# A two-part f32 kernel: the last output tiles of its first attention layer split into latent and context parts, and products of ones ahead of the input's transposes

## The chip, the cores and the metric

The kernel runs on one core of a Trainium2 chip. The metric is the device time of one execution in microseconds, as the median of several runs. In the text PE is the matmul engine (TensorE), PEld its weight loads, DVE is VectorE, ACT is ScalarE, POOL is GpSimd, and SP is the engine whose queue issues most of the DMA. PSUM is the accumulator memory of PE, in eight banks (`ps[:, 0]` to `ps[:, 7]`).

## The reference, cut to what matters

The whole computation is a gated block and after it two attention layers, A and B, on 512 latent tokens (`x`) and 256 context tokens (`ctx`), 1024 channels. The change lies at the start of the first block (norm of the input) and between the layers:

```python
for i in range(2):                                   # layer 0 is mixer A, layer 1 mixer B
    h  = modulate(x,   g_norm, shift,   scale)       # rmsnorm(x, g) * (1 + scale) + shift
    hc = modulate(ctx, g_norm, shift_c, scale_c)
    y, yc = mixer(h, hc, ...)
    x = x + gate[:, None] * y
    if not last:
        ctx = ctx + gate_c * yc
# end of mixer A:   y = (o * silu(g)) @ w_o ;  yc = (oc * silu(gc)) @ w_o
# start of mixer B: cq, ckv, kr, g = split(h @ w_in) ; ckv_c, kr_c = hc @ w_in[:, part]
```

The norm of a token needs the squares of all of its 1024 channels, so nothing of `h` can be made before the last output tile of mixer A is there.

## The kernel before

**Layout and precision.** Activations lie transposed, channels in the 128 partitions and tokens along the row, in KT = 8 tiles of 128 channels. Each f32 product is made of three fast ones: both operands are split in a high and a low part (`w_hi`, `w_lo`, `h_hi`, `h_lo`), and high by high, high by low and low by high are accumulated in PSUM. The high part of a weight strip (128x2048, 256 output channels) is a copy on ACT (helper `hi`, L748), the low part a difference on POOL in pieces of 512 columns (helper `lo`, L1267). There are two slots of `raw`, `w_hi` and `w_lo`. `hi` waits on `s_proj` until the slot's last products are done.

**Start.** ACT squares the four tiles of the input (L764), DVE and ACT make the norm's root and scale the tiles, and PE turns them with 32 transposes (L2164) after two small turns of parameter rows (L2155, L2156), which wait for the small loads (`s_const`). The transposes go over two token halves for k = 0 to 7, twice: the eighteenth is the first that completes a channel tile. ACT then makes `h_hi` tile by tile (L778), DVE `h_lo` (L1459), and PE the first projection (L2182 to L2184).

**End of layer A.** For each of eight output tiles m (phase `a_out`, L2565 to L2581) PE issues for each of 8 channel tiles three products of 512 columns (latent) and three of 256 (context), into banks 2j and 2j + 1 with j = m % 2, and signals `s_proj` once. DVE adds the tile to the residuals `x1T` (L1979) and `xcT` (L1980) and signals `s_free`; ACT squares both (L1111, L1112, helper `e_square`), and DVE sums the squares up to tile 6 (L1973, L1974, `s_esum`). ACT places the high parts of the next strips between the squares.

**Norm and layer B.** After the eighth tile PE sums over channels (L2586, helper `e_stat`: one-column products of `e_sum`, `e_csum` and the last squares with `ones`), DVE makes mean and reciprocal (L1987 to L1989), ACT the root (L1127), and PE spreads the roots over the partitions with transposes (L2390, helper `spread`). Then `h` of layer B is made tile by tile: DVE multiplies (L1772, `mod_t`), ACT scales and shifts twice, once into PSUM and once rounded into `h_hi` (L987, L988, `mod_hi`; for k = 0, 3, 6 DVE does the first, L1775), DVE subtracts into `h_lo` (L1780, `mod_lo`). PE takes each tile k as it comes, with six products of 512 columns for two output tiles of `cq` (L2449 to L2451, `weigh3`), then the latent products of the second strip of phase `b_in`, then those of the context.

The order on each engine is the order in which the code is written; there is no scheduler. Semaphores carry counts: phase objects (`Phase`, L518 to L520) hold the count at which a phase starts (`t0`).

Of the kernel before, what the change touches and what calls it, by code (L numbers as in the profile page):

```python
# [112 lines left out]
def block_kernel(nc, t):  # L113

    ctx = ExitStack()
    with ctx:
# [622 lines left out]
        def _(act):  # L739
# [367 lines left out]
            def e_square(k):  # L1107
# [15 lines left out]
            for k in range(5, KT):
                e_square(k)
            hi(b_in, 0, 1)
            act.wait_ge(s_einv, 1)
            nc.scalar.activation(e_st[:, 2, :], e_st[:, 1, :], ACT.Sqrt).then_inc(s_eroot, 1)  # L1127
            for k in range(KT):
                mod_hi(2 * KT + k, k, S, h_hi[:, k, :], 1, 0)
# [306 lines left out]
        def _(dve):  # L1436
# [532 lines left out]
            def e_sums(k):  # L1969
# [3 lines left out]
                v.tensor_tensor(e_sum[:, :], e_sum[:, :], tmp[:, k % 2, :], ALU.add)  # L1973
                v.tensor_tensor(e_csum[:, :], e_csum[:, :], e_csq[:, k % 2, :], ALU.add).then_inc(s_esum, 1)  # L1974

            for k in range(KT):
                j = k % 2
                dve.wait_ge(s_proj, a_out.t0 + k + 1)
                v.scalar_tensor_tensor(x1T[:, k, :], ps[:, 2 * j, :], ada_a[:, 2, k, 0:1], x1T[:, k, :], ALU.mult, ALU.add)  # L1979
                v.scalar_tensor_tensor(xcT[:, k, :], ps[:, 2 * j + 1, 0:C], ada_a[:, 2, k, 1:2], xcT[:, k, :],  # L1980
                                       ALU.mult, ALU.add).then_inc(s_free, 1)
# [851 lines left out]
```

## Time and profile before

| | us |
|---|---|
| median of 3 runs | 1522.52 |
| the three runs | 1522.37, 1522.52, 1525.46 |
| the profiled execution | 1521.91 |
| its span on the core | 1520.1 |
| PE busy | 1467.2 (97% of the span) |
| DVE, ACT, POOL busy | 788.6, 670.2, 556.8 |
| mean granted clock of PE | 0.989 of full speed |

The span is what the trace covers, from the first instruction to the last; 1.8 us of the profiled execution lie around it. In a timeline row, the first number is the start in us from the span's start, the second the duration of the merged rows, and what stands in brackets is how long the engine had been idle and what ended that. PEclk is the granted clock of PE: 1.00 is 2.4 GHz, 0.50 is 1.2 GHz. A row `x8` merges eight records. An f32 product that is not a transpose leaves two records, so that four products are `x8`.

### The profile page before, as it was taken

What the parts mean: (1) busy time and instruction counts of PE and PEld (TensorE: products, weight loads), DVE (VectorE), ACT (ScalarE), POOL (GpSimd) and SP (SyncE); (2) the same over time, 40 slices, a digit from 0 to 9 for tenths busy, and PEclk for the clock granted to TensorE, in tenths of its full rate; (3) what the DMA queues carried; (4) which work ended last, traced back from release to release, by engine and by line L of the source; (5) the groups of instructions that cost most, each with busy time, mean ns of one, the idle gap of its engine ahead of it and who ended that gap; (6) DMA issues with size and microseconds to landing.
All of it is one profiled execution on the core that took longest, in us unless ns stands there. A gap on an engine that the chain in (4) does not pass through costs nothing.

```text
span 1520.1 us, 22036 instructions
## 1 busy us (share of the span) xinstructions
PE 1467.2 (97%) x8808; PEld 1242.2 (82%) x8808; DVE 788.6 (52%) x1498; ACT 670.2 (44%) x1105; POOL 556.8 (37%) x488
## 2 busy tenths in 40 slices
PE   6999999999999999999999999999998999999997
PEld 5888898888887888888788898777787887888876
DVE  2868458177386423560277411777713636555533
ACT  6334243333433242123452131777722536777752
POOL 2534233234334365435443233333442142231241
PEclk9999999999999999999999999999999999999999
DMA  6533314223322135532321110021011130100111
GB/s 223 179 113 112 111 58 155 94 79 116 84 75 65 56 127 178 176 129 97 111 83 56 56 65 28 21 77 22 12 57 49 53 80 18 19 14 5 56 56 56
DMA packets 134918, 122.48 MB, mean 81 GB/s; under 512 B 17844, under 2 KB 130624, under 8 KB 134816
## 3 DMA queue, kind: packets, MB, share of 16 engines
q1 hardware_dynamic: 134702, 121.04, 25.4%
q8 instruction: 70, 1.15, 0.3%
q14 instruction: 32, 0.26, 0.1%
q10 hardware_dynamic: 114, 0.03, 0.0%
HBM read 116.60 MB, written 2.10 MB: 78 GB/s over the span
## 4 chain that ended last, share of the span: by engine, by line
PE 82%; DVE 12%; ACT 2%; issue 2%; POOL 0%; SPq 0%; DMA 0%; DVEq 0%; ACTq 0%
PE ps L2214 10%; PE ps L2216 10%; PE ps L2215 10%; PE ps L2716 3%; PE ps L2275 3%; PE ps L2705 3%; PE ps L2435 3%; PE ps L2434 3%; PE ps L2538 3%; PE ps L2436 3%; PE ps L2303 2%; DVE q_two L1512 2%; PE ps L2206 2%; PE ps L2529 2%; PE ps L2207 2%
## 5 line engine op out<-in xcount | busy, mean ns | idle before, releaser
L1267 POOL TENSOR_TENSOR w_lo<-raw,w_hi 128x512 fp32r<-128x512 f32 x320 | 422.5, 1351 | 648.3 <-ACT w_hi L748 633.2
L2214 PE MATMUL ps<-h_hi,w_hi 128*128 128x512 f32 x632 | 253.6, 401 | 8.0 <-DVE u_g L1713 4.5
L2215 PE MATMUL ps<-h_lo,w_hi 128*128 128x512 f32 x632 | 247.6, 392 | 0.0
L2216 PE MATMUL ps<-h_hi,w_lo 128*128 128x512 f32 x632 | 247.6, 392 | 0.0
L748 ACT ACTIVATE w_hi<-raw 128x2048 fp32r<-128x2048 f32 (+1 forms) x77 | 145.5, 1890 | 126.4 <-PE ps L2216 52.3
L2214 PEld LDWEIGHTS ps<-h_hi,w_hi 128*128 128x128 f32 x632 | 119.7, 189 | 36.9 <-issue 12.0
L2216 PEld LDWEIGHTS ps<-h_hi,w_lo 128*128 128x128 f32 x632 | 119.5, 189 | 25.8
L2215 PEld LDWEIGHTS ps<-h_lo,w_hi 128*128 128x128 f32 x632 | 119.9, 190 | 23.6 <-issue 0.2
L2100 DVE CUSTOM_DVE_ANT_0 prob_b<-ps,no_mask 128x768 f32<-128x768 f32 x64 | 61.3, 958 | 38.0 <-PE ps L2695 36.9
L2206 PE MATMUL ps<-w_hi,h_hi 128*128 128x256 f32 x256 | 73.6, 287 | 0.0
L2207 PE MATMUL ps<-w_lo,h_hi 128*128 128x256 f32 x256 | 72.4, 283 | 0.0
L2208 PE MATMUL ps<-w_hi,h_lo 128*128 128x256 f32 x256 | 72.4, 283 | 0.0
L1922 DVE CUSTOM_DVE_ANT_0 prob<-ps,mask_a,sink_neg 128x256 f32<-128x256 f32 (+2 forms) x80 | 53.4, 687 | 24.4 <-PE ps L2518 24.3
L1071 ACT ACTIVATE prob<-prob,m_neg 128x256 f32<-128x256 f32 (+2 forms) x96 | 64.9, 678 | 2.3 <-DVE m_neg L1922 2.0
L1179 ACT ACTIVATE pT_b<-ps 128x512 f32<-128x512 f32 x96 | 51.8, 592 | 26.1 <-PE ps L2705 25.8
L1410 POOL TENSOR_TENSOR q_bl<-q_raw,q_bh 128x512 fp32r<-128x512 f32 x16 | 20.7, 1292 | 112.9 <-ACT q_bh L1198 112.9
L1171 ACT ACTIVATE prob_b<-prob_b,m_neg 128x768 f32<-128x768 f32 x64 | 59.5, 930 | 1.5 <-DVE m_neg L2100 1.1
L2705 PE MATMUL ps<-ident,prob_b 128*128 128x128 f32 x384 | 50.6, 275 | 0.5 <-ACT pT_b L1179 0.5
L2206 PEld LDWEIGHTS ps<-w_hi,h_hi 128*128 128x128 f32 x256 | 49.0, 192 | 1.3 <-issue 1.2
L2529 PE MATMUL ps<-ident,prob 128*128 128x128 f32 x352 | 47.4, 275 | 2.6 <-DVE pT L1929 1.8
L2207 PEld LDWEIGHTS ps<-w_lo,h_hi 128*128 128x128 f32 x256 | 49.1, 192 | 0.0
L2208 PEld LDWEIGHTS ps<-w_hi,h_lo 128*128 128x128 f32 x256 | 49.1, 192 | 0.0
(460 smaller groups left out, 3524.0 us busy)
## 6 DMA issues: line engine op xcount, KB each, us to landing
raw<-in_w_in_dram SPq DMA_DIRECT2D x32, 1024.0 KB
raw<-in_ada_w_dram SPq DMA_DIRECT2D x12, 1024.0 KB
raw<-in_a_w_in_dram SPq DMA_DIRECT2D x10, 1024.0 KB
raw<-in_w_in_dram SPq DMA_DIRECT2D x16, 512.0 KB
ada_strip<-in_ada_w_dram SPq DMA_DIRECT2D x7, 1024.0 KB, 6.6
ada_half<-in_ada_w_dram SPq DMA_DIRECT2D x10, 512.0 KB, 3.6
raw<-in_b_w_in_dram SPq DMA_DIRECT2D x5, 1024.0 KB
raw<-in_w_proj_a_dram SPq DMA_DIRECT2D x4, 1024.0 KB
```

Source lines behind the costliest of these rows:

```text
L748: nc.scalar.activation(w_hi[:, ph.w(s), c], raw[:, s % 2, c], ACT.Copy).then_inc(s_hi, 1)
L1071: nc.scalar.activation(p, p, ACT.Exp, bias=m_neg[:, u:u + 1], scale=-1.0, accum_out=p_sum[:, u:u + 1]).then_inc(s_aexp, 1)
L1267: last = nc.gpsimd.tensor_tensor(w_lo[:, ph.w(s), p], raw[:, s % 2, p], w_hi[:, ph.w(s), p].bitcast(F32), ALU.subtract)
L2100: v.tensor_tensor_reduce(out=prob_b[n % 8][:, :], in0=src, in1=no_mask[:, 0:1].to_broadcast([P, ALL]), scale=-float(B_QK) ** -0.5, scalar= ...
L2206: mm(out, h_hi[:, k, tk], wh[:, k, :], start=(k == 0), stop=False)
L2207: mm(out, h_hi[:, k, tk], wl[:, k, :], start=False, stop=False)
L2208: last = mm(out, h_lo[:, k, tk], wh[:, k, :], start=False, stop=(k == KT - 1))
L2214: mm(ps[:, j, :], wh[:, k, c], xh[:, k, :], start=(k == 0), stop=False)
L2215: mm(ps[:, j, :], wh[:, k, c], xl[:, k, :], start=False, stop=False)
L2216: last = mm(ps[:, j, :], wl[:, k, c], xh[:, k, :], start=False, stop=(k == KT - 1))
L2529: last = nc.tensor.transpose(o, prob[(4 * x + h) % 8][:, b * P:(b + 1) * P], ident[:, :])
L2705: last = nc.tensor.transpose(ps[:, 4 + c % 2, u * P:(u + 1) * P], prob_b[(4 * x + u) % 8][:, b * P:(b + 1) * P], ident[:, :])
```

## The change

**Start.** Before it waits for the parameter rows, PE waits for `ones` and for the first squares of ACT, and then issues twenty f32 products of `ones` with `ones` (128x128 each) into bank 6, which nobody reads.

**End of layer A.** Output tiles 0 to 3 are as before. Tiles 4 to 7 issue their latent products alone; the context products of tiles 4, 5, 6 and 7 (`out_ctx`) follow, each with its own count of `s_proj` (`b_in.t0 += KT // 2`) and its own add (`add_ctx`), square (`e_square_ctx`) and sum (`e_sum_ctx`). The latent statistics stand behind `out_ctx(4)`, the spread of the latent roots behind `out_ctx(5)`. The context's statistics stand in the middle of the `cq` products of layer B, its spread ahead of their last tile.

**Layer B.** `h` is made in the order 2, 3, 4, 5, 6, 7, 0, 1 (`B_ORDER`), with the context's adds, sums and squares between its steps. The high part of `b_in`'s first strip stands on ACT behind the latent root, where it was ahead of the last three squares; that of the second stands in the middle of `h` and has 1280 columns in place of 2048. No product, square or add is added but the twenty of ones.

The core of the diff (DVE's and ACT's loops over `B_ORDER` are told by the rows below):

```diff
         b_in = Phase(a_out, 1, ("cq", "kv"))
+        b_in.t0 += KT // 2
...
+        B_ORDER = (2, 3, 4, 5, 6, 7, 0, 1)
+        KV_COLS = slice(0, KT * (B_KVR + B_ROPE))
...
+            pe.wait_ge(s_ones, 1)
+            pe.wait_ge(s_sq, 1)
+            for n in range(20):
+                mm(ps[:, 6, 0:P], ones[:, :], ones[:, :], start=True, stop=True)
             pe.wait_ge(s_const, N_CONST)
...
-                            for o, t0, t1 in ((ps[:, 2 * j, :], C, ALL), (ps[:, 2 * j + 1, 0:C], 0, C)):
+                            for o, t0, t1 in (lat, ctx_) if it == 0 else (lat,):
...
+            out_ctx(4)
+            pe.wait_ge(s_esum, KT - 2)
             e_stat(0, e_sum, NT)
-            e_stat(NT, e_csum, NC)
             pe.wait_ge(s_esq, KT)
-            e_stat(NT + NC, tmp[:, (KT - 1) % 2, :], NT)
-            e_stat(2 * NT + NC, e_csq[:, (KT - 1) % 2, :], NC).then_inc(s_estat, 1)
+            e_stat(NT, tmp[:, (KT - 1) % 2, :], NT).then_inc(s_estat, 1)
+            out_ctx(5)
             pe.wait_ge(s_eroot, 1)
-            spread(4, 0, [e_st[:, 2, n:n + 1] for n in range(NT)])
-            spread(5, C, [e_st[:, 2, NT + n:NT + n + 1] for n in range(NC)]).then_inc(s_espread, 1)
+            spread(4, 0, [e_st[:, 2, n:n + 1] for n in range(NT)]).then_inc(s_espread, 1)
+            out_ctx(6)
+            out_ctx(7)
 
             pe.wait_ge(s_lo, b_in.k(0, 0) + 1)
```

PE at the end of layer A, before (`a_hi` and `a_lo` are the gated attention output, `ones`, `e_sum`, `e_csum`, `tmp` and `e_csq` belong to the statistics, `e_st` holds the roots):

```order
L2580 MATMUL ps<-a_hi_132,w_lo 128x512
L2578 MATMUL ps<-a_hi_132,w_hi 128x256
L2579 MATMUL ps<-a_lo,w_hi 128x256
L2580 MATMUL ps<-a_hi_132,w_lo 128x256
L2586 MATMUL ps<-ones,e_sum 128x1 [waits s_esum,s_free]
L2586 MATMUL ps<-ones,e_sum 128x1 x3
L2586 MATMUL ps<-ones,e_csum 128x1 x2
L2586 MATMUL ps<-ones,tmp 128x1 [waits s_esq]
L2586 MATMUL ps<-ones,tmp 128x1 x3
L2586 MATMUL ps<-ones,e_csq 128x1 x2
L2390 MATMUL ps<-ident,e_st 128x128 [waits s_eroot]
L2390 MATMUL ps<-ident,e_st 128x128 x5
```

All 12 columns of statistics are issued there in one piece, and the spread of all six roots follows. PE in the change, around the latent statistics and around the latent spread (line numbers are those of the changed file; L2654 to L2656 are the context products of `out_ctx`):

```order
L2656 MATMUL ps<-a_hi_132,w_lo 128x256
L2661 MATMUL ps<-ones,e_sum 128x1 [waits s_esum]
L2661 MATMUL ps<-ones,e_sum 128x1 x3
L2661 MATMUL ps<-ones,tmp 128x1 [waits s_esq]
L2661 MATMUL ps<-ones,tmp 128x1 x3
L2654 MATMUL ps<-a_hi_131,w_hi 128x256
...
L2656 MATMUL ps<-a_hi_132,w_lo 128x256
L2452 MATMUL ps<-ident,e_st 128x128 [waits s_eroot]
L2452 MATMUL ps<-ident,e_st 128x128 x3
L2654 MATMUL ps<-a_hi_131,w_hi 128x256 [waits s_free]
```

Behind the last product of 512 columns there stand now two context tiles with the statistics between them, and two more behind the spread. On ACT, from the squares of the last tiles to the first tiles of `h`, before:

```order
L1112 ACTIVATE e_csq<-xcT 128x256
L748 ACTIVATE w_hi<-raw 128x2048 [waits s_proj,s_raw0]
L1111 ACTIVATE tmp<-xT 128x512 [waits s_esum,s_free]
L1112 ACTIVATE e_csq<-xcT 128x256
L1111 ACTIVATE tmp<-xT 128x512 [waits s_esum,s_free]
L1112 ACTIVATE e_csq<-xcT 128x256
L1111 ACTIVATE tmp<-xT 128x512 [waits s_esum,s_free]
L1112 ACTIVATE e_csq<-xcT 128x256
L748 ACTIVATE w_hi<-raw 128x2048 [waits s_proj,s_raw1]
L1127 ACTIVATE e_st<-e_st 128x6 [waits s_einv]
L988 ACTIVATE h_hi<-tmp,ada,mods 128x512 [waits s_mt]
```

The copy into `w_hi` for layer B's first strip is ahead of the last three pairs of squares. The same stretch of ACT in the change:

```order
L1117 ACTIVATE e_csq<-xcT 128x256
L1115 ACTIVATE tmp<-xT 128x512 [waits s_esum,s_free] x4
L1123 ACTIVATE e_csq<-xcT 128x256 [waits s_esum,s_free]
L1135 ACTIVATE e_st<-e_st 128x4 [waits s_einv]
L752 ACTIVATE w_hi<-raw 128x2048 [waits s_proj,s_raw0]
L1123 ACTIVATE e_csq<-xcT 128x256 [waits s_esum,s_free]
L991 ACTIVATE ps<-tmp,ada,mods 128x512 [waits s_mlo,s_mt]
L992 ACTIVATE h_hi<-tmp,ada,mods 128x512
L1123 ACTIVATE e_csq<-xcT 128x256 [waits s_esum,s_free]
L992 ACTIVATE h_hi<-tmp,ada,mods 128x512 [waits s_mt]
```

The copy into `w_hi` has moved from ahead of the last squares to behind the root of 4 columns, and the context's squares stand between the tiles of `h_hi`.

## Rows read from the trace of the kernel before

**Rows 1.** Busy time on the page, section 1: us, share of span, instructions

```profile
PE 1467.2 (97%) x8808; PEld 1242.2 (82%) x8808; DVE 788.6 (52%) x1498; ACT 670.2 (44%) x1105; POOL 556.8 (37%) x488
```

**Rows 2.** Waits of PE: in total, times, longest, us

```profile
PE ps L2155 <- DMA vec_rows<-in_b_kv_norm_dram: 13.6, 1, 13.6
...
PE ps L2449 <- DVE h_lo L1780: 4.1, 3, 3.0
```

**Rows 3.** Timeline of the start: start us, us, engine, line

```profile
5.99 0.19 ACT L764 ACTIVATION_READ_ACCUMULATOR xT<-x_tok 128x1 f32 x1
...
13.58 0.28 PE L2155 MATMUL ps<-ident,ln_rows 16*128 16x16 f32 x1 [13.58 <-DMA vec_rows<-in_b_kv_norm_dram]
...
14.05 5.58 PE L2164 MATMUL ps<-ident,x_tok 128*128 128x128 f32 x32
...
14.26 4.67 POOL L1276 TENSOR_TENSOR w_lo<-raw,w_hi 128x1024 fp32r<-128x1024 f32 x2 [13.25 <-ACT w_hi L760]
...
18.20 4.73 ACT L778 ACTIVATE h_hi<-ps,vec 128x512 fp32r<-128x512 f32 x8 [3.07 <-PE ps L2164]
...
19.91 0.47 PE L2182 MATMUL ps<-h_hi,w_hi 128*128 128x512 f32 x1 [0.27 <-DVE h_lo L1459]
```

**Rows 4.** Windows of L2164 alone: stretch, us, PE busy (x), PEld busy (x), PEclk, DMA

```profile
16.00:17.00 1.00, 1.00 (x6) 1.00 (x5) 1.00 1.10 348
...
18.00:19.00 1.00, 1.00 (x11) 1.00 (x10) 1.00 0.09 32
```

**Rows 5.** Timeline of PE at 433, four f32 products as eight records

```profile
433.30 1.05 PE L2353 MATMUL ps<-wsT,vs 128*128 128x128 f32 x8
```

**Rows 6.** Timeline of PE around the end of the first layer

```profile
1164.82 0.40 PE L2578 MATMUL ps<-a_hi,w_hi 128*128 128x512 f32 x1
...
1165.52 0.28 PE L2578 MATMUL ps<-a_hi,w_hi 128*128 128x256 f32 x1
...
1165.87 0.40 PE L2578 MATMUL ps<-a_hi,w_hi 128*128 128x512 f32 x1
...
1166.80 0.28 PE L2580 MATMUL ps<-a_hi,w_lo 128*128 128x256 f32 x1
...
1169.34 1.02 PE L2586 MATMUL ps<-ones,e_sum 128*128 128x1 f32 x8 [2.26 <-DVE e_csum L1974]
...
1173.47 1.54 PE L2390 MATMUL ps<-ident,e_st 128*128 128x128 f32 x6 [1.02 <-ACT e_st L1127]
...
1178.06 0.77 PE L2449 MATMUL ps<-h_hi,w_hi 128*128 128x512 f32 x1 [3.04 <-DVE h_lo L1780]
...
1189.74 0.50 PE L2449 MATMUL ps<-h_hi,w_hi 128*128 128x512 f32 x1
```

**Rows 7.** Windows of all engines: PE, PEld, DVE, ACT, POOL busy (x), PEclk, DMA, GB/s

```profile
1178.00:1182.00 4.00, 3.94 (x10) 3.16 (x11) 3.54 (x6) 3.03 (x5) 0.00 (x0) 0.51 0.68 236
```

**Rows 8.** Timeline of DVE in the same stretch

```profile
1167.12 0.75 DVE L1979 SCALAR_TENSOR_TENSOR xT<-ps,ada,xT 128x512 f32<-128x512 f32 x1 [6.32 <-PE ps L2580]
...
1172.56 0.18 DVE L1987 TENSOR_REDUCE ps<-ps 128x6 f32<-128x12 f32 x1 [2.76 <-PE ps L2586]
...
1175.05 0.69 DVE L1772 TENSOR_TENSOR tmp<-xT,ps 128x512 f32<-128x512 f32 x1 [1.87 <-PE ps L2390]
...
1177.23 0.68 DVE L1780 TENSOR_TENSOR h_lo<-ps,h_hi 128x512 fp32r<-128x512 f32 x1
...
1190.75 1.39 DVE L1994 COPY cq<-ps 128x512 f32<-128x512 f32 x2 [1.07 <-PE ps L2451]
```

**Rows 9.** Timeline of ACT, high part of the next layer's first strip

```profile
1150.38 1.92 ACT L748 ACTIVATE w_hi<-raw 128x2048 fp32r<-128x2048 f32 x1 [6.34 <-PE ps L2580]
```

**Rows 10.** Timeline of POOL, low part of the same strip

```profile
1152.38 5.03 POOL L1267 TENSOR_TENSOR w_lo<-raw,w_hi 128x512 fp32r<-128x512 f32 x4 [11.77 <-ACT w_hi L748]
```

**Rows 11.** Windows elsewhere: a gap before a low clock, and one without

```profile
786.00:789.00 3.00, 3.00 (x16) 3.00 (x16) 0.00 (x0) 0.14 (x1) 3.00 (x3) 0.50 0.00 0
...
957.00:962.00 5.00, 2.73 (x15) 1.91 (x13) 2.74 (x10) 3.36 (x8) 0.00 (x0) 1.00 0.00 0
```

More of the change, by code:

```diff
@@ L1119, in _ @@
             hi(a_out, 1, 1)
-            for k in range(3, 5):
+            for k in range(3, KT):
                 e_square(k)
+            e_square_ctx(4)
+            act.wait_ge(s_einv, 1)
+            nc.scalar.activation(e_st[:, 2, 0:NT], e_st[:, 1, 0:NT], ACT.Sqrt).then_inc(s_eroot, 1)
             hi(b_in, 0, 0)
[L1123 to L1129, printed above, removed]
+            e_square_ctx(5)
+            for n, k in enumerate(B_ORDER):
+                if n == 1:
+                    e_square_ctx(6)
+                if n == 3:
+                    e_square_ctx(7)
+                    hi(b_in, 0, 1, None, KV_COLS)
+                if n == 6:
+                    act.wait_ge(s_proj, b_in.t0)
+                if n == 7:
+                    act.wait_ge(s_einv, 2)
+                    nc.scalar.activation(e_st[:, 2, NT:NT + NC], e_st[:, 1, NT:NT + NC], ACT.Sqrt).then_inc(s_eroot, 1)
+                mod_hi(2 * KT + n, k, S, h_hi[:, k, :], 1, 0)
             for j in range(2):
@@ L1972, in e_sums @@
                     dve.wait_ge(s_esum, k - 1)
[L1973 to L1981 removed]
+                last = v.tensor_tensor(e_sum[:, :], e_sum[:, :], tmp[:, k % 2, :], ALU.add)
@@ new lines, in e_sums, with e_sum_ctx, add_lat @@
+                if k < KT // 2:
+                    last = v.tensor_tensor(e_csum[:, :], e_csum[:, :], e_csq[:, k % 2, :], ALU.add)
+                last.then_inc(s_esum, 1)
+            def e_sum_ctx(k):
+                dve.wait_ge(s_esq, k + KT // 2 + 1)
+                dve.wait_ge(s_esum, k + 2)
+                v.tensor_tensor(e_csum[:, :], e_csum[:, :], e_csq[:, k % 2, :], ALU.add).then_inc(s_esum, 1)
+            def add_lat(k):
+                dve.wait_ge(s_proj, a_out.t0 + k + 1)
+                return v.scalar_tensor_tensor(x1T[:, k, :], ps[:, 2 * (k % 2), :], ada_a[:, 2, k, 0:1], x1T[:, k, :], ALU.mult, ALU.add)
@@ L1987, in _ @@
-            link(v.tensor_reduce(st, ps[:, 5, 0:2 * (NT + NC)].rearrange("p (a c) -> p c a", a=2), AX.X, ALU.add))
-            link(v.tensor_scalar(st, st, 1.0 / D, EPS, ALU.mult, ALU.add))
-            v.reciprocal(e_st[:, 1, :], st).then_inc(s_einv, 1)
+            e_inverse(0, 0, NT)
+            e_sum_ctx(4)
+            add_ctx(5).then_inc(s_free, 1)
             dve.wait_ge(s_espread, 1)
-            modulate(2 * KT, range(KT), x1T, S, ada_b, 0, ps[:, 4, :], h_lo, h_hi)
+            root, i0 = ps[:, 4, :], 2 * KT
@@ new lines, in _ @@
+            mod_t(i0, B_ORDER[0], x1T[:, B_ORDER[0], :], S, ada_b, 0, root)
+            for n, k in enumerate(B_ORDER):
+                if n + 1 < KT:
+                    mod_t(i0 + n + 1, B_ORDER[n + 1], x1T[:, B_ORDER[n + 1], :], S, ada_b, 0, root)
+                mod_lo(i0 + n, h_lo[:, k, :], h_hi[:, k, :], S)
+                if n == 0:
+                    add_ctx(6).then_inc(s_free, 1)
+                    e_sum_ctx(5)
+                if n == 1:
+                    add_ctx(7).then_inc(s_free, 1)
+                if n == 2:
+                    e_sum_ctx(6)
+                if n == 5:
+                    dve.wait_ge(s_estat, 2)
+                    e_inverse(3 * NT, NT, NC)
@@ L2581, in _, with out_ctx @@
                         last.then_inc(s_proj, 1)
-            pe.wait_ge(s_free, b_in.t0)
-            pe.wait_ge(s_esum, KT - 2)
+            def out_ctx(m):
+                s, j = m // 2 % 2, m % 2
+                if m >= 6:
+                    pe.wait_ge(s_free, a_out.t0 + m + KT // 2 - 1)
+                wh, wl, c = k_of(w_hi, s), k_of(w_lo, s), slice(j * P, (j + 1) * P)
+                o = ps[:, 2 * j + 1, 0:C]
+                for k in range(KT):
+                    xh, xl = a_hi(k)[:, 0:C], a_lo[:, k, 0:C]
+                    mm(o, wh[:, k, c], xh, start=(k == 0), stop=False)
+                    mm(o, wh[:, k, c], xl, start=False, stop=False)
+                    last = mm(o, wl[:, k, c], xh, start=False, stop=(k == KT - 1))
+                last.then_inc(s_proj, 1)
             def e_stat(c, x, n_tok):
```

53 lines of the change are left out of this document (44 added, 9 removed).

## The prediction

> **What bounds the kernel now.** I read the busy times first: PE is busy 97% of the span [rows 1], so a change is worth only what it takes from PE's idle time or from stretches in which its clock is low. Then PE's waits: the largest is the 13.6 us at the start, until the parameter rows have landed, and the next of the change's reach are those on `h_lo`, 4.1 us in three waits [rows 2]. Then the timeline of these two places, where the reader is to look at the starts of PE's rows.
>
> At the start the 32 transposes take from 14.05 to 19.6 us [rows 3]. They don't go at one pace: 6 or 7 begin in a microsecond up to 18.0, eleven in the one after [rows 4]. The seven of 17 and 16 us stand about 0.213 us apart, the later ones about 0.11 us. The column PEclk says 1.00 in both stretches, but half the pace for the same instruction is the lower level, 1.2 GHz, and the rise comes 4.4 us after PE's first work at 13.58.
>
> Between the layers the last product of layer A begins at 1166.80, the statistics at 1169.34, the spread at 1173.47 and the first product of layer B at 1178.06 [rows 6]. In these 11.1 us PE does 24 one-column records and 6 transposes. The clock falls meanwhile, and the next 4 us run at 0.51, with 10 matmuls where the higher level fits twice as many [rows 7]. DVE and ACT work through a chain (add, square, statistics, root, spread, multiply, split) of which nothing overlaps with PE's products.
>
> **The start, step by step.** The first squares end at 6.18 (5.99 + 0.19, [rows 3]), so the ones start at 6.2. An f32 product is two records; eight such records stand (1.05 - 0.275)/7 = 0.111 us apart at the higher level, 0.275 us being the duration of one [rows 5], and I double that for the lower, 0.22, as six transposes of that level do: (1.54 - 0.42)/5 = 0.22 [rows 6]. If the rise comes again 4.4 us after the first work, at 10.6, then 20 of the 40 records have gone, and the other 20 take 2.2 us: done at 12.8. That is 0.8 us ahead of 13.58, so that they delay nothing, and the idle 0.8 us is short. The first complete channel tile needs two small turns and 18 transposes. Before, ACT's first `h_hi` starts at 18.20 [rows 3]. At the higher level the eighteenth starts at 13.8 + 17 x 0.11 = 15.7, and ACT 0.5 us later (as now, 17.68 to 18.20): 16.2. That is 2.0 us earlier. From there `h_hi` to the first product takes 1.7 us [rows 3], and the low parts of the weights are no obstacle: the first half is there at 14.26 + 2.3 = 16.6, against a first product at 17.9; the second half at 18.93, against 20.6. After that PE's order is unchanged and everything shifts: **-2.0 us**. Bounds: if the clock hasn't risen when the parameter rows land, 40 records end at 6.2 + 8.8 = 15.0 and the eighteenth transpose comes 0.6 us later than now, +0.6; the other end is a gain of 2.1, with transposes at 0.109.
>
> The Trainium skill (TensorE: Matmul & The Clock Gate, Part 1: The HAM clock gate) says that the number of matmuls which one and the same kernel issues at the lower level differs from run to run (6, 11 or 14 in its measurement), and advises against fitting to one count. By it the rise at 10.6 is not sure; what a late rise would make of the time is the bound above. The trace before holds one execution and can't show the spread.
>
> **Between the layers, PE's side.** Three 512-column products take 0.70 us (1164.82 to 1165.52), three of 256 take 0.35 (to 1165.87) [rows 6], so a whole tile takes 8 x 1.05 = 8.40, its latent half 5.60, its context half 2.80. The last tile ends at 1166.92, tile 4 so starts at 1133.3. In the change, on the same scale: four latent halves to 1155.7, context 4 to 1158.5. The last latent add and square follow their tile: add from 1155.9 (0.75 [rows 8]), square 0.63 to 1157.4, both before 1158.5. So the latent statistics need no wait; 16 records x 0.11 = 1.8, to 1160.3. Context 5 to 1163.1. Meanwhile DVE makes mean and reciprocal in 0.6 us and ACT the root (1172.56 to 1173.42 before [rows 8, 6]), by 1161.5, so the spread of four at 1163.1 also waits for nothing; to 1163.6. Contexts 6 and 7 to **1169.2**.
>
> What is late next is the weight strip. `hi` of layer B's first strip must wait until context 5 has read the slot, since slot 0 serves tiles 4 and 5. Before it ran at 1150.38 for 1.92 us, and POOL's low part from 1152.38 for 5.03 [rows 9, 10], long hidden. Now it starts at 1163.4, ACT ends at 1165.3 and POOL at **1170.4**. PE waits 1.2 us for it. The copy also holds back ACT's first `h_hi`, queued behind it: DVE's first multiply can start at 1163.9, but ACT's two passes run from 1165.7 to 1167.1, and the first `h_lo` is there at 1167.9, still ahead of 1170.4.
>
> **Between the layers, DVE's and ACT's side.** Before, the eight tiles went at (1189.74 - 1178.06)/7 = 1.67 us each [rows 6], paced by DVE and ACT, and PE needs only 6 x 0.234 = 1.40. In the change the two engines carry beside it: on DVE two adds, two sums and the second inverse (0.48 + 0.42 + 0.48 + 0.42 + 0.6 = 2.4 us), on ACT three squares, a copy of 1280 columns and a root (3 x 0.4 + 1.2 + 0.2 = 2.6). Following the written order with these durations, I get `h_lo` at 1167.9, 1170.2, 1171.8, 1174.7, 1175.9, 1177.9, 1180.6 and 1182.2. PE: three tiles from 1170.4 to 1174.7, the fourth and fifth to 1177.6, context statistics 0.9, the sixth to 1179.9, a wait of 0.8, the seventh to 1182.1, spread 0.3, the eighth to **1183.8**. Before, the eighth tile starts at 1189.74 and is issued by 1191.2. So **-7.4 us**. What follows (copies of `cq`, the context's `h`, the strip of 1280 columns, whose low part is ready at 1175.7) hangs on the eighth tile as before.
>
> Bounds: without any wait PE would be through at 1169.2 + 11.2 + 0.9 + 0.3 = 1181.6, a gain of 9.6; if each of the eleven inserted operations costs a semaphore's trip of 0.2 us on the path, the gain is 5.2.
>
> **Sum.** 1521.9 - 2.0 - 7.4 = 1512.5 for an execution like the profiled one; the median of the runs lies 0.6 higher: **1513.1**.
>
> **Rivals.** (1) The clock falls in the filled stretch nevertheless. For it: a stretch of 2 us without products before 786 is followed by 3 us at 0.50 [rows 11], and here stand 1.8 us of one-column records and a wait of 1.2. Against it: around 957 to 962 PE was busy 2.73 of 5 us and the clock stayed at 1.00 [rows 11]. Price: 3 us at half pace, as from 786 to 789, lose 1.5: 1514.6; six us at half pace lose 3: 1516.1.
>
> (2) The ones bring no rise in time: +0.6 in place of -2.0, 1515.7. Against it speaks only that PE's dense work at 13.58 brought the rise in 4.4 us.
>
> (3) The reordering hides nothing, because the root still comes late or the statistics wait for the context: only the start remains, 1522.5 - 2.0 = 1520.5, within 0.2%. The order of the counts speaks against it.
>
> (4) Slower: the interleaved chain of layer B's norm serialises. The queues of DVE and ACT hold context work that waits for PE ahead of the tiles of `h`; if each tile then pays the unhidden trip of the first one, 1175.05 to 1178.06 = 3.0 us [rows 8, 6], and a little more for its insert (3.5 in all), the eighth tile is through at 1170.4 + 7 x 3.5 + 1.4 = 1196.3, 5.1 later than now, and PE, idle more than half of that, stays at the lower level for a while (+1.9 as in [rows 7]): 1522.5 - 2.0 + 7.0 = 1527.5. It decides from a pace of (1193.2 - 1.4 - 1170.4)/7 = 3.1 us a tile; the pace measured is 1.67.
>
> **Chances.** The forecast has 0.80 (its own range 1511 to 1514.5), rival (1) 0.08, (2) 0.06, (3) 0.03, (4) 0.03. Range: down by the 2.2 us of PE without any wait, up to the loss of 2.2 by trips or to rival (2): 1510.8 to 1516.2. A measurement of this kernel can tell about 0.2%, 3 us, from no change. Faster 0.94, same 0.03, slower 0.03.
>
> **What would show it.** Right: transposes at 0.11 us from the first on, and `h_hi` at 16.2; a gap of about 1 us before PE's first product of layer B, ended by POOL's `w_lo`; that product some 9.6 us earlier (7.6 on the unshifted scale); granted clock 1.00 through it. Wrong: transposes that begin after 13.9; a low clock after the latent statistics; `h_lo` as the releaser of most tiles; an end of the first layer's context later than four halves.

## The result, and the profile after

| | before | change |
|---|---|---|
| median of the runs, us | 1523.99 (4 runs) | 1511.55 (4 runs) |
| lowest and highest | 1522.37 to 1526.99 | 1509.71 to 1512.82 |
| the profiled execution, its span | 1521.91, 1520.1 | 1512.08, 1510.3 |

The ratio is 0.9921, with a 95% interval of 0.9904 to 0.9938, so the change is faster, by 0.8%. The forecast was 1513.1 in 1510.8 to 1516.2. The profiled executions differ by 9.8 us, where 9.4 were forecast; the medians differ by 12.4, and by 12.9 when both were run again (1522.5 and 1509.6, see below). Lines of the changed file are some 60 to 90 higher than those of before.

The start of the change, as a timeline (start us, us, engine, line). It answers to [rows 3]:

```profile
5.98 7.55 PE L2215 MATMUL ps<-ones 128*128 128x128 f32 x40 [5.98 <-ACT xT L768]
...
13.46 0.23 PE L2217 MATMUL ps<-ident,ln_rows 16*128 16x16 f32 x1
...
13.78 3.66 PE L2226 MATMUL ps<-ident,x_tok 128*128 128x128 f32 x32
...
16.00 3.00 ACT L782 ACTIVATE h_hi<-ps,vec 128x512 fp32r<-128x512 f32 x5 [0.95 <-PE ps L2226]
...
17.70 0.47 PE L2244 MATMUL ps<-h_hi,w_hi 128*128 128x512 f32 x1 [0.27 <-DVE h_lo L1479]
```

The ones stand where PE had waited. The transposes take 3.66 us in place of 5.58, and `h_hi` and the first projection come 2.2 us earlier than in [rows 3] (16.00 against 18.20, 17.70 against 19.91).

PE between the layers. The last row is the eighth tile of `h`, and it answers to [rows 6]:

```profile
1157.09 0.95 PE L2661 MATMUL ps<-ones,e_sum 128*128 128x1 f32 x8
1157.90 1.03 PE L2661 MATMUL ps<-ones,tmp 128*128 128x1 f32 x8
...
1161.75 0.60 PE L2452 MATMUL ps<-ident,e_st 128*128 128x128 f32 x4
...
1167.81 0.28 PE L2656 MATMUL ps<-a_hi,w_lo 128*128 128x256 f32 x1
1169.27 0.50 PE L2681 MATMUL ps<-h_hi,w_hi 128*128 128x512 f32 x1 [1.18 <-POOL w_lo L1287]
...
1181.31 0.50 PE L2681 MATMUL ps<-h_hi,w_hi 128*128 128x512 f32 x1
```

Neither the statistics nor the spread waits; what is left of the 11.1 us is a rest of 1.18 us behind the last context product, ended by POOL's low part. The strip's copy on ACT, POOL's part, and DVE's first, seventh and eighth `h_lo` (they answer to [rows 8], [rows 9] and [rows 10]):

```profile
1162.01 1.92 ACT L752 ACTIVATE w_hi<-raw 128x2048 fp32r<-128x2048 f32 x1 [2.20 <-PE ps L2656]
```
```profile
1164.00 5.21 POOL L1287 TENSOR_TENSOR w_lo<-raw,w_hi 128x512 fp32r<-128x512 f32 x4 [24.20 <-ACT w_hi L752]
```
```profile
1165.74 0.69 DVE L1800 TENSOR_TENSOR h_lo<-ps,h_hi 128x512 fp32r<-128x512 f32 x1 [1.22 <-ACT h_hi L992]
...
1178.89 0.68 DVE L1800 TENSOR_TENSOR h_lo<-ps,h_hi 128x512 fp32r<-128x512 f32 x1
1180.57 0.69 DVE L1800 TENSOR_TENSOR h_lo<-ps,h_hi 128x512 fp32r<-128x512 f32 x1 [0.99 <-ACT h_hi L992]
```

Windows of all engines (PE, PEld, DVE, ACT, POOL busy, PEclk, DMA, GB/s), here and at 960:

```profile
1165.00:1169.00 4.00, 3.09 (x26) 2.89 (x25) 3.26 (x5) 2.05 (x4) 4.00 (x4) 1.00 0.00 0
1169.00:1173.00 4.00, 3.73 (x16) 3.11 (x17) 3.70 (x7) 4.00 (x6) 1.42 (x2) 1.00 0.68 187
...
960.00:964.00 4.00, 3.78 (x18) 2.99 (x20) 2.44 (x10) 3.42 (x13) 0.66 (x3) 0.61 0.00 0
```

The clock stays at 1.00 through the boundary, where it was 0.51 [rows 7], while DVE and ACT are busy 3.7 and 4.0 of 4 us. But at 960 it now falls to 0.61; before it stayed up there [rows 11].

**Where the 9.8 us arose.** The same two products of PE in both kernels, one ahead of the boundary and one well behind it; first before, then the change:

```profile
1091.61 0.66 PE L2529 MATMUL ps<-ident,prob 128*128 128x128 f32 x4 [0.46 <-DVE pT L1929]
...
1272.21 0.47 PE L2660 MATMUL ps<-ckv_hi,w_hi 128*128 128x512 f32 x1 [1.52 <-POOL w_lo L1267]
```
```profile
1090.73 0.44 PE L2591 MATMUL ps<-ident,prob 128*128 128x128 f32 x2 [0.46 <-DVE pT L1949]
...
1263.77 0.47 PE L2750 MATMUL ps<-ckv_hi,w_hi 128*128 128x512 f32 x1 [1.52 <-POOL w_lo L1287]
```

The shift is 2.2 at the first projection, 2.5 at the first scores of layer A (957.54 against 960.00), 0.9 at 1091 (the low clock at 960 costs 1.6), and 8.4 behind the boundary. The stretch over the boundary took 180.60 us and takes 173.04: **7.6 us** less. This distance is the measure of the experiments below, since nothing that happens outside of it changes it, and inside of it no trace has a low clock except at the boundary. The last 1.4 us come behind it, where before has another low stretch (its window from 1277, and in the change the window of the same work, from 1268):

```profile
1277.00:1281.00 4.00, 3.76 (x13) 3.24 (x14) 2.14 (x6) 1.78 (x4) 0.00 (x0) 0.57 0.06 11
```
```profile
1268.00:1272.00 4.00, 3.21 (x21) 2.93 (x22) 3.17 (x8) 2.28 (x5) 0.00 (x0) 1.00 0.01 1
```

### The profile page after: what moved, and what is told of

Same layout as the page of the kernel before. It is cut to its first block, busy times and chain, and to the rows that moved or that the text cites. A ratio compares the mean times of both kernels' runs of the same rounds, so it can differ in the third digit from the quotient of the medians.

```text
span 1510.3 us, 22129 instructions
## 1 busy us (share of the span) xinstructions
PE 1469.5 (97%) x8848; PEld 1245.4 (82%) x8848; DVE 792.9 (53%) x1501; ACT 670.0 (44%) x1106; POOL 555.5 (37%) x487
## 4 chain that ended last, share of the span: by engine, by line
PE 82%; DVE 12%; ACT 3%; issue 2%; POOL 0%; DMA 0%; DVEq 0%; SPq 0%; ACTq 0%
PE ps L2276 10%; PE ps L2278 10%; PE ps L2277 10%; PE ps L2806 3%; PE ps L2337 3%; PE ps L2795 3%; PE ps L2600 3%; PE ps L2497 3%; PE ps L2496 3%; PE ps L2498 3%; PE ps L2365 2%; PE ps L2591 2%; DVE q_two L1532 2%; PE ps L2268 2%; PE ps L2269 2%
## 5 line engine op out<-in xcount | busy, mean ns | idle before, releaser
L1287 POOL TENSOR_TENSOR w_lo<-raw,w_hi 128x512 fp32r<-128x512 f32 (+1 forms) x319 | 421.1, 1351 | 639.8 <-ACT w_hi L752 624.7
L752 ACT ACTIVATE w_hi<-raw 128x2048 fp32r<-128x2048 f32 (+2 forms) x77 | 144.9, 1882 | 122.4 <-PE ps L2278 52.3
```

What stands on the lines that cost most here:

```text
L752: nc.scalar.activation(w_hi[:, ph.w(s), c], raw[:, s % 2, c], ACT.Copy).then_inc(s_hi, 1)
L1287: last = nc.gpsimd.tensor_tensor(w_lo[:, ph.w(s), p], raw[:, s % 2, p], w_hi[:, ph.w(s), p].bitcast(F32), ALU.subtract)
```

## The experiments

### Each half alone

The kernel before with the twenty products of ones:

```diff
+            pe.wait_ge(s_ones, 1)
+            pe.wait_ge(s_sq, 1)
+            for n in range(20):
+                mm(ps[:, 6, 0:P], ones[:, :], ones[:, :], start=True, stop=True)
             pe.wait_ge(s_const, N_CONST)
```

> The kernel before, with the twenty products of ones alone. Theory (they raise the clock ahead of the transposes, and the whole of the kernel then shifts): transposes about 0.11 us apart from the first on, first projection at 17.7 to 17.9 in place of 19.9, total 2.0 to 2.2 us under the kernel before, give or take 1.6 for a low stretch of the clock that may come or go elsewhere. The gap between the layers and its low clock as before. Rival (the shift is taken back by a later wait for a DMA): first projection at 17.8, but the first layer's output at the old time, total within 0.5 of the kernel before.

Measured: 1521.33 us (1518.39 to 1523.09, 10 runs) against 1522.53; ratio 0.9988, interval 0.9978 to 0.9999. The start does what it does in the change, and then the boundary (PE's timeline, then two windows):

```profile
13.86 3.66 PE L2168 MATMUL ps<-ident,x_tok 128*128 128x128 f32 x32
17.79 0.47 PE L2186 MATMUL ps<-h_hi,w_hi 128*128 128x512 f32 x1 [0.28 <-DVE h_lo L1459]
...
1167.11 1.41 PE L2590 MATMUL ps<-ones,e_sum 128*128 128x1 f32 x8 [2.26 <-DVE e_csum L1974]
```
```profile
1168.00:1172.00 4.00, 3.94 (x19) 3.85 (x19) 0.00 (x0) 0.80 (x1) 3.12 (x3) 0.50 0.00 0
1172.00:1176.00 4.00, 1.54 (x6) 1.14 (x6) 1.98 (x5) 0.96 (x2) 1.81 (x2) 0.50 0.23 36
```

The statistics start 2.2 us earlier than in [rows 6], so the shift is still whole there. But their eight records take 1.41 us in place of 1.02: the clock, which before had still been up at the statistics, is already low. The distance over the boundary is 182.24 (1089.39 to 1271.63), 1.6 more than before. Nothing was edited there. Whether the earlier start moved the fall or executions differ there by themselves, one trace of each can't tell.

The change without the twenty products:

```diff
-            for n in range(20):
-                mm(ps[:, 6, 0:P], ones[:, :], ones[:, :], start=True, stop=True)
```

> The change without the ones. Theory (the two parts add up): start as before, 19.9 for the first projection; the eighth tile of the cq products is through 7.4 us earlier than before relative to tile 4's start; total 7.5 under the kernel before, give or take 1.6. Rival (the split's gain needs the clock phase that the ones set): a low stretch at the context statistics, and 4 to 6 us only.

Measured: 1513.54 us (1511.66 to 1513.97, 4 runs), ratio 0.9933 (0.9907 to 0.9959). The distance is 172.99 (1092.04 to 1265.03), the wait for `w_lo` 1.18 us. The split gives its 7.6 us without the ones. By the medians the halves are worth 1.2 and 9.0 us, by the ratios 1.8 and 10.2; the intervals (1.6 and 4 us to either side) are too wide to tell this from the profile's 2.2, less the 1.6, and 7.6. Its start is not that of the kernel before, though nothing differs there:

```profile
14.05 4.93 PE L2222 MATMUL ps<-ident,x_tok 128*128 128x128 f32 x32
```

Here the pace doubles some 3 us after PE's first work at 13.58, not 4.4, and the first projection is at 19.27. So without the ones the start varies by 0.6 us too, and what they are worth is 1.6 to 2.2.

### How many ones

```diff
-            for n in range(20):
+            for n in range(10):
```

> The change with ten products of ones in place of twenty. They end near 10.3 at the lower level, 3 us ahead of the parameter rows. Theory (what raises the clock is dense work right up to the transposes): the rise doesn't come in time or the level falls again, the transposes go at 0.21 for most of their length and the first projection is 1.0 to 2.1 later than in the change (18.7 to 19.9). Rival (any dense work of 4 us is enough and a rest of 3 us is harmless): first projection at 17.8 as in the change.

Measured: 1513.95 us (1511.21 to 1514.37, 4 runs), ratio 0.9936 (0.9915 to 0.9957). PE at the start, and a window:

```profile
6.22 4.61 PE L2215 MATMUL ps<-ones 128*128 128x128 f32 x20 [6.22 <-ACT xT L768]
14.10 0.23 PE L2217 MATMUL ps<-ident,ln_rows 16*128 16x16 f32 x1 [3.27 <-DMA vec_rows<-in_b_kv_norm_dram]
...
14.52 5.17 PE L2226 MATMUL ps<-ident,x_tok 128*128 128x128 f32 x32
```
```profile
14.00:17.00 3.00, 2.90 (x14) 2.87 (x15) 0.37 (x2) 1.76 (x2) 2.11 (x1) 0.53 1.12 334
```

Twenty records are over at 10.8. They took 4.61 us, 0.22 us each, so all of them went at the lower pace: the ones ended before the clock had risen. PE then rests 3.3 us, and when the parameter rows are there the transposes begin at half pace (PEclk 0.53), 5.17 us for the 32. The first projection is at 19.96, as late as without any ones (19.91 [rows 3], 19.27 in the kernel above); 0.5 of that is that the parameter rows landed later here. The medians can't tell ten ones from twenty, since the intervals overlap; the traces of the start can.

Forty products:

```diff
-            for n in range(20):
+            for n in range(40):
```

> The change with forty products of ones. Theory: 80 records, some 24 at 0.21 and the rest at 0.11, end at 6.0 + 5.1 + 6.2 = 17.3, the small turns and transposes start 3.7 later than in the change at the higher level; first projection at 21.4 to 21.6, 3.8 later; total 3.8 over the change. Rival (the start has slack that hides a late transpose): total within 1.5 of the change, that is no more than a low stretch.

Measured: 1514.57 us (1512.78 to 1516.01, 4 runs), ratio 0.9946 (0.9927 to 0.9965).

```profile
6.49 12.02 PE L2215 MATMUL ps<-ones 128*128 128x128 f32 x80 [6.49 <-ACT xT L768]
...
18.76 3.66 PE L2226 MATMUL ps<-ident,x_tok 128*128 128x128 f32 x32
22.69 0.47 PE L2244 MATMUL ps<-h_hi,w_hi 128*128 128x512 f32 x1 [0.27 <-DVE h_lo L1479]
```

The transposes are as fast as in the change but 5.0 us later (3.7 were expected; the ones began 0.5 later, and some 27 records, not 24, went at the lower pace): the ones are no free filler once they outlast the wait. Of the 5.0 the median shows 3.0; the profiled execution has less low clock at 460 than the change's. Of the three numbers tried, twenty fits the wait best: it ends at 13.53 when the clock rises late, just where the parameter rows land. Numbers between were not tried.

### What covers the norm: the statistics behind all context tiles

```diff
             add_ctx(4).then_inc(s_free, 1)
+            add_ctx(5).then_inc(s_free, 1)
             dve.wait_ge(s_estat, 1)
             e_inverse(0, 0, NT)
             e_sum_ctx(4)
-            add_ctx(5).then_inc(s_free, 1)
...
-            out_ctx(4)
+            for m in range(4, KT):
+                out_ctx(m)
             pe.wait_ge(s_esum, KT - 2)
...
-            out_ctx(5)
             pe.wait_ge(s_eroot, 1)
...
-            out_ctx(6)
-            out_ctx(7)
```

> The change with the latent statistics and spread behind all four context tiles (DVE adds context tile 5 ahead of them): same work, nothing of the norm's chain beside it. Theory (the gain is that the chain runs beside context products): PE stands still or does little for about 6 us behind the last context tile (statistics 1.8, inverse and root 0.9, spread 0.5, first tile of h 3.0), its first product of layer B is 4.5 to 5.5 later than in the change, the clock falls there; total 4 to 7 over the change, so 3 to 6 under the kernel before. Rival (the order of the tiles and the later weight strip matter, not the overlap; PE is paced by DVE and ACT anyway): within 1.5 of the change.

Measured: 1518.5 us (1516.82 to 1521.56, 10 runs), ratio 0.9966 (0.9954 to 0.9978). The distance is 180.31 (1090.43 to 1270.74): all but 0.3 of the 7.6 us is gone. (The median is 4.0 below the kernel before, where the start and the 0.3 give 2.5; the trace has no low stretch near 1277, which is worth 1.4.) PE:

```profile
1168.19 0.73 PE L2452 MATMUL ps<-ident,e_st 128*128 128x128 f32 x4 [0.93 <-ACT e_st L1135]
...
1175.19 0.80 PE L2679 MATMUL ps<-h_hi,w_hi 128*128 128x512 f32 x1 [6.26 <-POOL w_lo L1287]
```

The rest is there again, and on the scale of the product ahead of the boundary the first product of layer B comes 6.2 us later than in the change, where 4.5 to 5.5 were expected. But the end of the rest is not the norm's: POOL's low part is late, since the strip's copy stands on ACT behind the root and the root is late. Two causes are mixed, so the next kernel takes one away by moving the copy ahead of the root:

```diff
+            hi(b_in, 0, 0)
             act.wait_ge(s_einv, 1)
             nc.scalar.activation(e_st[:, 2, 0:NT], e_st[:, 1, 0:NT], ACT.Sqrt).then_inc(s_eroot, 1)
-            hi(b_in, 0, 0)
```

> As the kernel with the latent statistics behind the four context tiles, but with the copy of the next strip's high part on ACT ahead of the latent root instead of behind it. This takes the strip out of the comparison and leaves the bare norm chain uncovered. Theory (the unhidden norm chain costs the time, the strip only masks it): the copy runs from about 1160 on, POOL's low part is ready by 1167, and the first product of layer B comes at about 1171.3 (1175.2 in the former), ended by h_lo and not by w_lo. The chain of h then begins about 5 us later than in the change; of the 7.6 us that the split gained, 4 to 6 are lost, and about 1.5 of that may be a low clock: 1515.5 to 1517.5. Rival A (the strip behind the root was the whole loss): 1511.5 to 1513, as the change. Rival B (DVE and ACT pace the tiles whatever starts them, and the clock falls as long): as the former, 1518.5, with the first product earlier but the eighth tile not.

Measured: 1518.0 us (1516.38 to 1519.87, 6 runs), ratio 0.9966 (0.9954 to 0.9979).

```profile
1167.20 0.83 PE L2452 MATMUL ps<-ident,e_st 128*128 128x128 f32 x4 [0.93 <-ACT e_st L1136]
1171.60 0.77 PE L2679 MATMUL ps<-h_hi,w_hi 128*128 128x512 f32 x1 [3.57 <-DVE xcT L2009]
```
```profile
1171.00:1175.00 4.00, 3.40 (x8) 2.75 (x9) 3.74 (x9) 3.47 (x6) 0.00 (x0) 0.50 0.00 0
```

On its own scale (product at 1088.7 against 1089.7 ahead of the boundary) the first product comes 2.6 us earlier, ended by DVE: the first `h_lo` and, right behind it, the add of context tile 6, whose bank the product takes. Yet the distance is 178.86 (1089.45 to 1268.31), only 1.5 better. With the late statistics the strip was worth 1.5 us, and the bare chain 5.8, within the theory's 4 to 6, though the time of 1518.0 lies 0.5 above its range. Rival A is refuted. Rival B can't be told apart by the median, and holds in part: the clock is low as long as in the kernel before this one, and DVE and ACT pace the tiles. The last kernel tells these apart. It fills the two rests, and nothing else:

```diff
             e_stat(NT, tmp[:, (KT - 1) % 2, :], NT).then_inc(s_estat, 1)
+            for n in range(4):
+                mm(ps[:, 2, 0:P], ones[:, :], ones[:, :], start=True, stop=True)
             pe.wait_ge(s_eroot, 1)
             spread(4, 0, [e_st[:, 2, n:n + 1] for n in range(NT)]).then_inc(s_espread, 1)
+            for n in range(16):
+                mm(ps[:, 2, 0:P], ones[:, :], ones[:, :], start=True, stop=True)
```

> As the kernel with the late statistics and the strip's copy ahead of the root, plus 4 f32 products of ones between the statistics and the spread, and 16 between the spread and the first product of layer B, into a bank that nobody reads then: they fill the rests of 1.2 and 4.0 us in which PE waits for the norm chain, and nothing else is changed. It tells what of the 5.8 us lost there is low clock. Theory: the products keep the granted clock at 1.00 from 1167 on, and yet little comes back, since the h_lo of the chain end at the same times (1171.1, 1173.4, 1175.0, 1177.7, 1178.9, 1181.1) and pace the tiles; only the context's statistics, which waited for PE's fifth tile, come some 1 us earlier and the last two tiles with them: eighth tile 96.1 us behind the point at 1088.7 (97.2 without the products, 91.3 in the change), 1516.9. Rival: the 14 products issued at 0.43 in place of 0.23 us cost their full 2.9 us: eighth tile 94.3 behind, 1515.1. Second rival: the clock falls nevertheless, 1518 or, with the products in the way, more.

Measured: 1515.98 us (1513.58 to 1520.43, 5 runs), ratio 0.9949 (0.9935 to 0.9964). The median lies between theory and rival, and the trace is of the slowest of the five, with more low clock near 780 and 960, so the distance decides: 177.95 (1092.70 to 1270.65), 0.9 better than without the products. The eighth tile stands 96.26 us behind the product at 1091.97 (theory 96.1, rival 94.3).

```profile
1170.95 3.74 PE L2675 MATMUL ps<-ones 128*128 128x128 f32 x32
...
1180.88 0.50 PE L2683 MATMUL ps<-h_hi,w_hi 128*128 128x512 f32 x1 [1.11 <-DVE h_lo L1800]
```
```profile
1175.00:1179.00 4.00, 3.79 (x16) 2.55 (x15) 3.73 (x7) 4.00 (x7) 0.30 (x1) 1.00 0.00 0
```

The clock is 1.00 all through, the products of layer B go at the full pace again, and PE now waits 1.11 us for an `h_lo` in the middle of the tiles. The low clock had been hidden behind DVE and ACT, all but 0.9 us. So the 7.6 us of the split are, in the order in which they were undone, 1.5 for the strip, 0.9 for the clock and 4.9 that are left for the norm's chain itself, with 0.3 that the late order keeps.

### The wait for the strip

POOL makes the low part in PE's order, in quarters with a count each, and PE waits for the quarter that a tile needs:

```diff
-            lo(b_in, 0, 0)
+            pool.wait_ge(s_hi, b_in.k(0, 0) + 1)
+            for a in (S, 2 * S, 3 * S, 0):
+                p = slice(a, a + S)
+                last = nc.gpsimd.tensor_tensor(w_lo[:, b_in.w(0), p], raw[:, 0, p], w_hi[:, b_in.w(0), p].bitcast(F32), ALU.subtract)
+                last.then_inc(s_piece if a else s_lo, 1)
...
-            pe.wait_ge(s_lo, b_in.k(0, 0) + 1)
             for n, k in enumerate(B_ORDER):
+                if n < 6:
+                    if n % 2 == 0:
+                        pe.wait_ge(s_piece, n // 2 + 1)
+                elif n == 6:
+                    pe.wait_ge(s_lo, b_in.k(0, 0) + 1)
```

> The change, but the low part of layer B's first strip is made in the order in which PE takes the tiles, and PE waits for each quarter of it alone. Takes the wait of 1.2 us for POOL away. Theory (DVE and ACT pace the eight tiles of h, the POOL wait costs little): first product 1.2 earlier, eighth tile 0.4 to 0.6 earlier, waits for h_lo grow by 0.6; total 0.5 under the change. Rival (the POOL wait is on the path with its full length): eighth tile 1.2 earlier.

Measured: 1511.81 us (1507.88 to 1512.17, 4 runs), ratio 0.9918 (0.9894 to 0.9943). The distance is 173.01 (1090.49 to 1263.50), the change's within 0.03. The longer wait of PE at this place, in its timeline:

```profile
1173.73 0.50 PE L2690 MATMUL ps<-h_hi,w_hi 128*128 128x512 f32 x1 [1.23 <-DVE h_lo L1805]
```

The wait of 1.18 us on POOL is gone and one of 1.23 on `h_lo` has come in its place. The wait for the strip cost nothing, and the prices put on its removal were too high.

### Rests in which the clock falls elsewhere

The low stretches at 456, 742, 783 and 960 in the change lie behind rests of PE of 1.7 to 3.8 us, and they come and go: the change, run again beside the last of the kernels below, had none at 742 and one of half the length at 456.

> The change itself once more, beside the next kernel. Theory: total 1510 to 1513; low stretches at 455, 742 and 783, and at one of 960 and 1268 or at none, according to how the rests fall, so that single executions differ by 1.5 or so.

Measured: 1509.6 us (1509.48 to 1511.67, 4 runs), ratio 0.9914 (0.9899 to 0.9929). Its profiled span is 1507.7, 2.6 below the first one's, at the same code, and its median lies below the range of the forecast. Now 16 products of ones (bank 6) fill the longest rest, at 453, ahead of the fourth chunk's gates:

```diff
+                    if (g, j) == (3, 0):
+                        for n in range(16):
+                            mm(ps[:, 6, 0:P], ones[:, :], ones[:, :], start=True, stop=True)
                     project(gates, it, s, j, False)
```

> The change, and sixteen further products of ones where PE stands still for 4.2 us at 452.6 (before the fourth channel group's projection in the gated block), into bank 6. 32 records at 0.111 are 3.55 us and fit. Theory (it is the rest that takes the clock; products of ones in it keep the higher level): the low stretch of 6.8 us from 455.7 is gone or halved, total 1.7 to 3.4 under the change, projection not delayed. Rival (the level falls for another reason, as load or time): low stretch stays, total as the change or up to 0.4 over it.

Measured: 1511.5 us (1508.32 to 1511.96, 4 runs), ratio 0.9922 (0.9903 to 0.9941): no gain, where 1.7 to 3.4 us were expected. Windows of it:

```profile
457.00:462.00 5.00, 4.94 (x22) 4.11 (x23) 1.38 (x2) 2.00 (x2) 4.00 (x4) 1.00 0.00 0
...
781.00:785.00 4.00, 4.00 (x19) 4.00 (x20) 0.63 (x4) 0.21 (x1) 4.00 (x4) 0.50 0.02 6
```

The clock is up at 457, as meant (0.50 over 456 to 462 in the change), but the low stretch near 781, behind an unfilled rest, is twice as long as in the change. In this execution a later rest took the saved time back. So three more rests get 8 products each (at 739 and 778 in bank 4, at 955 ahead of layer A's first scores in bank 6), all in this form:

```diff
+            for n in range(8):
+                mm(ps[:, 6, 0:P], ones[:, :], ones[:, :], start=True, stop=True)
             a_scores(0, 0)
```

> As gap1, and eight products of ones each (1.8 us) in the three rests of 2.1 us at 739.4 (ahead of the third pair of context transposes), 777.8 (ahead of the input norm's statistics) and 955.5 (ahead of the first scores). Theory: the four low stretches of the change go (6.8 + 3 x 3.4 = 17 us at half pace, of which one or two may stay), total 5 to 8.5 under the change. Rival (two of the stretches come from one-column statistics and transposes that wait, which ones beside them don't help): 455.7 and 960.8 go, 742 and 783 stay, 3.4 to 5 under the change.

Measured: **1508.16 us** (1508.11 to 1508.23, 4 runs), ratio 0.9904 (0.9889 to 0.9920). This is 3.4 us under the change's first median and 1.4 under its second, less than the 5 to 8.5 of the theory. The stretches at 456, 742 and 960 are gone from its trace, that at 780 stays, and a new one stands at 1264. And then 6 and 8 more at 1262 and 1265, ahead of the second channel block of layer B's up projection, where gap4's trace had a low stretch of its own:

```diff
+                if m == 1 and part < 2:
+                    for n in range((6, 8)[part]):
+                        mm(ps[:, 6, 0:P], ones[:, :], ones[:, :], start=True, stop=True)
```

> The four fills of gap4 and two more in the second layer, six and eight products of ones in the rests of 1.8 us and 2.3 us ahead of the second pair's key products (1256.6 and 1261.2 in gap4), into bank 6. Theory (the rests take the clock): the low stretch at 1263.9 of gap4 goes too, only the one at the input norm's statistics (779) and the tail stay low; total 1505.5 to 1507, 1.5 under gap4's 1508.2 and 4 to 6 under the change. Rival (the stretch at 1264 comes from elsewhere or the fills delay the key products, which wait for POOL and DVE): as gap4 or up to 1 over it.

Measured: **1505.09 us** (1504.88 to 1507.74, 4 runs), ratio 0.9881 (0.9864 to 0.9897). It beats the kernel before by 1.2% and the change, run beside it (1509.6), by 4.5 us; their intervals don't overlap. The profiled execution is the slowest of the four (1507.74). Part of why is at its start, where the parameter rows landed 1.4 us later than in the change:

```profile
14.84 0.23 PE L2217 MATMUL ps<-ident,ln_rows 16*128 16x16 f32 x1 [2.25 <-DMA vec_rows<-in_b_kv_norm_dram]
```

The transposes behind this rest of 2.25 us still take 3.66 us, as in the change. Windows of the change run again, and of this kernel:

```profile
457.00:462.00 5.00, 5.00 (x17) 4.01 (x18) 1.38 (x2) 1.77 (x1) 4.00 (x4) 0.72 0.00 0
...
959.00:963.00 4.00, 4.00 (x21) 2.96 (x20) 1.65 (x7) 3.42 (x11) 1.73 (x3) 0.68 0.00 0
```
```profile
457.00:462.00 5.00, 4.74 (x26) 3.94 (x25) 2.06 (x3) 3.17 (x4) 3.05 (x3) 1.00 0.00 0
...
781.00:785.00 4.00, 4.00 (x24) 4.00 (x23) 0.00 (x0) 0.17 (x1) 4.00 (x4) 0.57 0.00 0
...
959.00:963.00 4.00, 4.00 (x30) 3.03 (x29) 3.19 (x11) 4.00 (x12) 2.54 (x4) 1.00 0.00 0
```

One low stretch stays within the kernel, from 781.4 (the clock also falls at 1498, where PE is done). The rest ahead of it is filled; what follows the ones there are 24 records of one and two columns, 2.7 us of them (PE's timeline):

```profile
775.49 1.95 PE L2484 MATMUL ps<-ones 128*128 128x128 f32 x16
777.35 1.95 PE L2488 MATMUL ps<-ones,x_sq 128*128 128x1 f32 x16
779.15 1.03 PE L2491 MATMUL ps<-fw,tmp 128*128 128x2 f32 x8
```

PE counts as busy there, and yet the clock falls. That such narrow products bring it down is a suspicion which no run tested; the 16 of the latent statistics didn't in the change.

## Why the prediction was right, step by step

**The start** was put at -2.0 and is -2.2 against this trace of the kernel before (-1.6 against the start of the kernel with the split alone). The transposes at 0.11 us from the first on were right (3.66 us for 32), and 0.12 us of the gain is that PE's first turn stands at 13.46 in place of 13.58, since the parameter rows landed that much earlier, which the change doesn't do. The step with luck in it is the rise, which was taken as 4.4 us after the first work. In the changed kernel it came after 5.9 us, with 27 records at the lower pace, and in its second run after some 3.1, with 14. Windows of the ones alone (the change, then the change again), the same microsecond:

```profile
10.00:11.00 1.00, 1.00 (x6) 1.00 (x6) 1.00 1.10 348
```
```profile
10.00:11.00 1.00, 1.00 (x12) 1.00 (x11) 1.00 1.10 344
```

The latest rise still ended the 40 records at 13.53, level with the parameter rows, and the earliest at 12.3, with a rest of 1.2 us in which the clock held. The sum was the same for both, and rival (2), no rise in time, is refuted for twenty products. One bound of this step was worked out wrong: with the ones done at 15.0 and the lower pace kept, the eighteenth transpose comes 1.4 us later than before (15.0 + 0.47 + 17 x 0.213 = 19.1 against 17.7), not 0.6. The Trainium skill (TensorE: Matmul & The Clock Gate, Part 1: The HAM clock gate) says that one kernel's count of slow matmuls differs from run to run and warns against fitting to one; the traces agree, with 14 and 27 records. That rule was the right reason to keep the upper bound.

**PE's side of the boundary** held step by step: the statistics and the spread wait for nothing, the last context product is followed by a wait on `w_lo`, forecast as 1.2 and measured as 1.18. On the scale of the prediction (add the 0.9 us by which PE is early there) the first product of layer B is at 1170.2 against 1170.4.

**DVE's and ACT's side.** The ends of the first, seventh and eighth `h_lo` are, on the same scale, 1167.3, 1180.5 and 1182.1 against 1167.9, 1180.6 and 1182.2, and the eighth tile is through at 1183.7 against 1183.8. The place gives 7.6 against 7.4. Following the written order of both queues with durations of the trace was worth its trouble: the low part in quarters and the filled rests show that these two queues, and neither the strip nor the clock, set the pace of the tiles.

**Rival (1)**, a low clock in the filled stretch, didn't happen at the boundary in any profiled execution that has the split as it is. **Rival (3)**, a reordering that hides nothing, is what the late statistics show: 0.3 us of the 7.6 were left, and the median was 1518.5, a ratio of 0.9966, where the price given was 1520.5. **Rival (4)** would have needed 3.1 us a tile; the tiles go at (1181.31 - 1169.27)/7 = 1.72.

**What the prediction didn't have** is the low clock elsewhere. It took everything behind the start as unchanged in length. But which rests were followed by a low stretch differed: one came at 960 (+1.6), one went at 1277 (-1.4), and in the kernel with the ones alone the boundary's grew (+1.6). The kernel with the split alone has the same two differences at 960 and 1277, so they don't need the earlier start. They nearly cancel in the profiled execution, so that the sum came out by luck as well as by its terms. The medians show it: they moved by 12.4 and 12.9 us, where the two parts give 9.8, and of all eight runs of the change the median is 1510.4, under the range. The mechanism stands, and about 3 us of the gain in the medians are none of its terms; that they are low stretches fits the traces, but was not shown run by run. Such a term belongs in the range, with 1.5 us for each stretch that may come or go. The range's upper end of 1516.2 also doesn't follow from the terms that it names, which give 1515.3 (trips) and 1515.7 (rival 2). Not tried: the natural order of the tiles, since the first two tiles of `h` lie in memory that the context products still read.

## What to carry to other kernels

Work that needs only part of a result (here the norm of the latent tokens) should be issued as soon as that part is there, with independent products behind it that cover its chain; count the cover against the chain, and then follow the queues of the helper engines in their written order, since they set what comes next. A weight strip or any other copy that waits for a slot belongs ahead of the chain's late step in its queue where that step is uncovered (1.5 us here); where the chain was covered, the wait for the strip cost nothing. Rests of PE of some 2 us and more can be filled with products that nobody reads, but one rest filled alone gave nothing and six gave 4.5 us; size each filling to end when the real work is ready, and judge by several runs.

## What the runs showed of the hardware

- At the start, twenty products of ones and rests of 0 to 2.25 us behind them left PE at the higher pace (3.66 us for 32 transposes); after ten products, all at the lower pace, and a rest of 3.3 us the transposes began at 0.53 and took 5.17. A rest of 1.2 us between the layers left the granted clock at 1.00.
- Whether a low stretch follows a rest doesn't depend on its length alone: behind the same rest of 1.78 us the clock stayed at 1.00 near 960 in the kernel before and fell to 0.61 in the change. Two executions of one kernel differ by 2.6 us.
- Six to sixteen products of 128x128 in each of six rests, 54 in all, took 4.5 us off a kernel whose PE was already busy 97% of the span.
- Half the clock for some ten us can cost little: where DVE and ACT set the pace, PE's slower products hid behind them, all but 0.9 us.
